# GpSimd makes all lower halves of the first 89 expert-up tiles, and VectorE passes each on behind its own step of expert choice

## The chip, the cores and the metric

The kernel runs on one core of a Trainium2 chip. The metric is the device time of one execution in microseconds (us). The kernel before took 4111.89 us (median of 3 runs, 4111.05 to 4112.73).

Five engines of the core work side by side: TensorE (PE; its weight loads are shown as PEld), VectorE (DVE), ScalarE (ACT), GpSimd (POOL), and SyncE (SP), which here only issues transfers. They meet at semaphores.

## The reference, cut to what matters

Four layers in a row, over 256 tokens of width 1024. Each is a mixer (RWKV-7 and pooling twice, a gated linear recurrence, latent attention) followed by a PEER feed-forward with 16384 experts. Only the feed-forward is touched by the change:

```
q = (h @ peer_q).reshape(B, S, 8, 2, 128)
scores = jnp.einsum('bshpd,hpkd->bshpk', q, peer_keys)
s, i = lax.top_k(scores, 16)                       # two lists of 16 for each head
cand_s = s[..., 0, :, None] + s[..., 1, None, :]   # 256 pair sums for each head
top_s, sel = lax.top_k(cand_s, 16)
gate = softmax(top_s)
act = gelu(einsum('td,ted->te', hx, u_sel))        # expert up
out = einsum('te,ted->td', gx * act, v_sel)        # expert down
```

The kernel does not gather the chosen experts. It multiplies the tokens by all 16384 rows of `peer_u`, in 128 tiles of 128 experts, and sets the unchosen ones to zero by a gate.

## The kernel before, in words

A weight tile of 128 x 1024 fp32 (512 KB) passes through four places. SP loads it into one of four `raw` buffers. ACT rounds it to `t_hi` (L707, the upper half). DVE or POOL makes the remainder `t_lo = raw - t_hi` (the lower half; L1195 on DVE, L617 on POOL). PE multiplies both. `t_hi` and `t_lo` have two buffers each, so the upper half of tile k starts once PE is through with tile k-2.

For the first 95 of the 128 expert-up tiles of a layer PE runs `merged`: 8 matmuls of 512 columns with `t_hi` (L2059), a wait for the lower half, then 8 matmuls of 256 columns with `t_lo` (L2067). Tile k needs a free PSUM bank too, that is, the sum of tile k-2 taken by DVE (L1780, semaphore `taken`).

Beside it, during the first 88 tiles, DVE chooses the experts: 44 steps for each of two halves of the tokens, one step to a tile. Steps 0 to 15 look for the largest 16 of 128 scores (instructions with one input); steps 16 and 17 form the pair sums (L1760, `tensor_tensor` over 1024 elements); steps 18 to 29 look for the largest 16 of 256 sums; step 30 prepares the softmax (L1831 to L1835, four short instructions); steps 31 to 42 are four look-ups, each of a comparison (L1768), a product (L1771) and a reduction (L1772); step 43 divides by the sum (L1843, short). In every step DVE first takes the sum of tile k-2 (`sum_of_tile`), then does the step (`choose`), then sees to a lower half (`lower_of_tile`).

Of the 88 tiles beside the choice, POOL makes the lower halves of the odd ones and DVE those of the even ones. PE waits on `lo_by_pool` for a tile of POOL's, and on `lo_done` for one of DVE's. `lo_done` counts all tiles in order, and SP waits on it before it loads the tile four further on. So DVE passes a tile of POOL's on: it waits for `lo_by_pool` and then raises `lo_done` by a tiny memset into `mark` (L1783). Behind the choice, POOL sets part of the arena to ones (L625) and makes gate columns (L631); DVE makes gate columns too (L1869).

Of the kernel before, what the change touches and what calls it, by code (L numbers as in the profile page):

```python
# [25 lines left out]
P = 128  # L26
# [3 lines left out]
TT = T // P  # L30
# [103 lines left out]
RANK_KEYS, PAIRS, RANK_PAIRS, SOFT, LOOK_UP, CHOSEN = 0, 16, 18, 30, 31, 43  # L134
STEPS = 44
LATE = TT * STEPS + 7
POOL_LOWERS = TT * STEPS // 2


def by_pool(k):  # L140

    return k % 2 == 1 and k < TT * STEPS
SMALL = {"mix0": 64, "mix1": 128, "mix2": 144, "mix3": 176}
NORMS_BEFORE = {"out0": 1, "out1": 3, "lout": 6, "wo": 8}
HSPLIT = {"ffn0": 3, "ffn1": 6, "ffn2": 9, "ffn3": 13, "wo": 11}
# [24 lines left out]
def in_loops(eng, name, a, b, body):  # L170

    tiles_in_loops(eng, SEGS[name][0] + a, b - a, lambda n, j, k, i: body(n, j, k + a, i))
# [63 lines left out]
def build(nc, x_in_dram, w_tiles, u_tiles, v_tiles, params, consts, lora, lru_w, mla_w, mla_uv, keys_t, pool_inv,  # L236
          positions, out):
    with ExitStack() as ctx:
        def sb(name, shape, dt=F32):
            return ctx.enter_context(nc.sbuf_tensor(name, shape, dt))  # L240

        def sem(name):
            return ctx.enter_context(nc.semaphore(name))
# [6 lines left out]
        x = sb("x", [P, DC, T])  # L250
        h_both = sb("h_both", [P, DC, 2, T], F32R)
        h_hi, h_lo = h_both[:, :, 0, :], h_both[:, :, 1, :]
        mark = sb("mark", [P, 1])
        par = sb("par", [P, NPAR])
        cst = sb("cst", [P, 4, P])
        mods = sb("mods", [P, 48])
# [35 lines left out]
        def act_slot(k, i):  # L292

            if i is None:
                return act_at[:, k // EB, :, k % EB, :]
            return act_at[:, bass.ds(i + k // EB, 1), :, k % EB, :].rearrange("p b q t -> p (b q) t")
# [6 lines left out]
        def by_quads(v):  # L303

            return v.rearrange("p (q t) -> p q t", t=4)
# [100 lines left out]
        lo_done = sem("lo_done")  # L406
        lo_by_pool = sem("lo_by_pool")
# [190 lines left out]
        def _(pool):  # L598
# [12 lines left out]
            def lower_halves(l):  # L611

                first = SEGS[f"u{l}"][0]
                for k in range(1, TT * STEPS, 2):
                    j = first + k
                    pool.wait_ge(hi_done, j + 1)
                    pool.tensor_tensor(t_lo[:, j % SPL, :], raw[:, j % RAW, :], t_hi[:, j % SPL, :].bitcast(F32),  # L617
                                       ALU.subtract).then_inc(lo_by_pool, 1)
# [42 lines left out]
            for l in range(4):  # L661
# [26 lines left out]
                pool.wait_ge(h_split, DC * HSPLIT[f"ffn{l}"])  # L688
                pool.dma_start(tk["keys"], keys_t[l]).then_inc(keys_in, 16)
                lower_halves(l)  # L690
                middle_hots(l)
                if l < 3:
# [494 lines left out]
        def _(dve):  # L1187
# [4 lines left out]
            def lower(n, j, name):  # L1192

                dve.wait_ge(hi_done, n + 1)
                tts(t_lo[:, j % SPL, :], raw[:, j % RAW, :], t_hi[:, j % SPL, :].bitcast(F32),  # L1195
                    ALU.subtract).then_inc(lo_done, 1)
# [577 lines left out]
            def sum_of_tile(l, k):  # L1774

                j = SEGS[f"u{l}"][0] + k
                if k >= 2:
                    dve.wait_ge(copied, LATE * l + k - 1)
                    slot = act_slot(k - 2, None)
                    tts(slot, by_quads(ps[:, j % 2, 0:T]), slot, ALU.add).then_inc(taken, 1)  # L1780
                if k and by_pool(k - 1):
                    dve.wait_ge(lo_by_pool, POOL_LOWERS * l + k // 2)
                    dve.memset(mark[:, :], 0.0).then_inc(lo_done, 1)  # L1783

            def lower_of_tile(l, k):

                if not by_pool(k):
                    lower(SEGS[f"u{l}"][0] + k, SEGS[f"u{l}"][0] + k, f"u{l}")

            def choose(l):  # L1790
# [11 lines left out]
                for tt in range(TT):  # L1802
                    for k in range(STEPS):
                        sum_of_tile(l, STEPS * tt + k)
                        if k < PAIRS:
                            if k % 4 == 0:
# [32 lines left out]
                        else:  # L1839
# [3 lines left out]
                            tts(e[:, 2], e[:, 2], tk["den"][:, 1, :].unsqueeze(2).broadcast_to([P, HEADS, TOPK]),  # L1843
                                ALU.mult).then_inc(chosen, 1)
                        lower_of_tile(l, STEPS * tt + k)
                a = TT * STEPS
                for k in range(a, a + 4):
                    sum_of_tile(l, k)
                    lower_of_tile(l, k)
                sel_out(1)  # L1850

            def gates(l):
# [34 lines left out]
                for k in range(TT * STEPS + 4, LATE + 2):  # L1887
                    sum_of_tile(l, k)
                    lower_of_tile(l, k)
                    if k == TT * STEPS + 4:  # L1890
                        dve.wait_ge(sel_ready, TT * (l + 1))
                        columns(0)
                    elif k == TT * STEPS + 5:
                        rows(0)
# [116 lines left out]
        def _(pe):  # L2011
# [37 lines left out]
            def merged(l, a, b):  # L2049

                name, first = f"u{l}", SEGS[f"u{l}"][0]

                def step(n, j, k, i):
                    pe.wait_ge(hi_done, n + 1)
                    pe.wait_ge(taken, k + (TAKEN[name] - 1))
                    hi = t_hi[:, j % SPL, :].rearrange("p (c m) -> p c m", c=DC)
                    lo = t_lo[:, j % SPL, :].rearrange("p (c m) -> p c m", c=DC)
                    for c in range(DC):
                        mm(ps[:, j % 2, :], hi[:, c, :], h_both[:, c, :, :].rearrange("p a t -> p (a t)"),  # L2059
                           start=(c == 0), stop=False)  # L2060
                    if by_pool(j - first):
                        at = POOL_LOWERS * l + (j - first) // 2 + 1
                        pe.wait_ge(lo_by_pool, at if i is None else i * 2 + at)
                    else:
                        pe.wait_ge(lo_done, n + 1)
                    for c in range(DC):
                        ins = mm(ps[:, j % 2, 0:T], lo[:, c, :], h_hi[:, c, :], start=False, stop=(c == DC - 1))  # L2067
                    ins.then_inc(tile_used, 1)
                in_loops(pe, name, a, b, step)
# [637 lines left out]
```

## Time and profile before

| | before |
|---|---|
| median of 3 runs | 4111.89 us |
| the profiled execution | 4110.32 us |
| its span | 4108.5 us |
| PE busy | 3973.6 us (97%) |
| DVE busy | 3062.8 us (75%) |
| ACT busy | 2336.6 us (57%) |
| POOL busy | 949.3 us (23%) |
| mean granted TensorE clock | 0.981 of full speed |

The 1.8 us between span and execution time lie outside the span. PE is the engine that sets the time; a share of busy time says nothing of a single stage, though, so the rows below are taken from the stage of the expert-up tiles. In layer 0 this lies between 294 and 575 us of the span; it comes four times.

### The profile page before, as it was taken

The page shows a single profiled execution, that of the slowest core. Times are in us where ns is not written, and L with a number is a line of the kernel's source. Part 1 is how long each engine was busy: PE and PEld are TensorE (multiplying, and loading weights), DVE is VectorE, ACT ScalarE, POOL GpSimd, SP SyncE. Part 2 cuts the span into 40 slices and gives each one's busy share as a digit, 9 for nine tenths or more (in the row PEclk, how much of TensorE's full clock was granted, in tenths as well). Part 3 has the DMA queues.
Part 4 walks back from the last instruction along what each step waited for, and adds up shares of the span by engine and source line. Part 5 has one row for each costly group of instructions (what it writes and reads, how often), then busy time and mean ns, then how long its engine had stood idle before and what let it go on. Part 6 is the DMA issues. An engine that isn't in the chain of part 4 may idle for free.

```text
span 4108.5 us, 76965 instructions
## 1 busy us (share of the span) xinstructions
PE 3973.6 (97%) x27046; PEld 3531.8 (86%) x27046; DVE 3062.8 (75%) x5383; ACT 2336.6 (57%) x4303; POOL 949.3 (23%) x646
## 2 busy tenths in 40 slices
PE   6999999999999999999998999999998999999999
PEld 6888889888889888988888988998887798898887
DVE  6758889767565888986766688987775578897555
ACT  4246578544534656854456566875454456686554
POOL 0104455000010444510000244531000034452000
PEclk9999999999999999999998999999998999999999
DMA  8345543878514554377853555358882255534664
GB/s 285 124 134 184 187 157 114 271 246 290 172 49 134 179 184 162 113 258 243 290 175 110 176 184 185 123 173 296 284 286 108 83 169 184 179 117 151 193 192 156
DMA packets 203683, 749.41 MB, mean 182 GB/s; under 512 B 22704, under 2 KB 23856, under 8 KB 202192
## 3 DMA queue, kind: packets, MB, share of 16 engines
q1 hardware_dynamic: 178416, 646.51, 47.1%
q0 software_dynamic: 25056, 100.15, 7.7%
q8 instruction: 125, 2.05, 0.2%
q14 instruction: 86, 0.70, 0.1%
HBM read 745.52 MB, written 1.05 MB: 182 GB/s over the span
## 4 chain that ended last, share of the span: by engine, by line
PE 88%; DVE 7%; ACT 3%; issue 1%; DMA 1%; POOL 1%; SPq 0%; DVEq 0%; ACTq 0%
PE ps L2059 15%; PE ps L2497 11%; PE ps L2504 11%; PE ps L2500 11%; PE ps L2067 8%; PE ps L2031 6%; PE ps L2032 6%; PE ps L2038 6%; PE ps L2480 6%; PE ps L2206 2%; DVE t_lo L1195 1%; ACT t_hi L707 1%; PE ps L2074 1%; DMA raw<-w_tiles 1%; PE ps L2455 1%
## 5 line engine op out<-in xcount | busy, mean ns | idle before, releaser
L707 ACT CAST t_hi<-raw 128x1024 fp32r<-128x1024 f32 x1180 | 1243.3, 1054 | 1004.6 <-PE ps L2504 694.4
L1195 DVE TENSOR_TENSOR t_lo<-raw,t_hi 128x1024 fp32r<-128x1024 f32 x1004 | 1229.3, 1225 | 686.2 <-ACT t_hi L707 667.8
L2059 PE MATMUL ps<-h_both,t_hi 128*128 128x512 f32 x3040 | 769.0, 395 | 10.9 <-DVE arena L1780 10.9
L2059 PEld LDWEIGHTS ps<-h_both,t_hi 128*128 128x128 f32 x3040 | 549.8, 190 | 111.2 <-issue 11.6
L2031 PE MATMUL ps<-h_both,t_hi 128*128 128x256 f32 x2304 | 603.7, 298 | 36.8 <-DVE h_both L1327 17.5
L617 POOL TENSOR_TENSOR t_lo<-raw,t_hi 128x1024 fp32r<-128x1024 f32 x176 | 453.6, 2577 | 744.0 <-ACT t_hi L707 744.0
L2032 PE MATMUL ps<-h_both,t_hi 128*128 128x256 f32 x2304 | 579.4, 287 | 0.0
L2497 PE MATMUL ps<-t_hi,h_both 128*128 128x512 f32 x2048 | 548.0, 389 | 5.4 <-DVE h_both L1919 5.4
L2504 PE MATMUL ps<-t_lo,h_both 128*128 128x512 f32 x2048 | 547.4, 389 | 0.0
L2500 PE MATMUL ps<-t_hi,h_both 128*128 128x512 f32 x2048 | 547.3, 389 | 0.0
L2031 PEld LDWEIGHTS ps<-h_both,t_hi 128*128 128x128 f32 x2304 | 451.2, 196 | 50.9 <-issue 34.6
L2497 PEld LDWEIGHTS ps<-t_hi,h_both 128*128 128x128 f32 x2048 | 383.9, 188 | 85.4 <-issue 6.1
L2067 PEld LDWEIGHTS ps<-h_both,t_lo 128*128 128x128 f32 x3040 | 412.2, 191 | 48.7 <-POOL t_lo L617 13.1
L2032 PEld LDWEIGHTS ps<-h_both,t_hi 128*128 128x128 f32 x2304 | 452.8, 197 | 1.2 <-issue 1.0
L2500 PEld LDWEIGHTS ps<-t_hi,h_both 128*128 128x128 f32 x2048 | 384.4, 188 | 79.9
L2504 PEld LDWEIGHTS ps<-t_lo,h_both 128*128 128x128 f32 x2048 | 384.4, 188 | 79.8
L2067 PE MATMUL ps<-h_both,t_lo 128*128 128x256 f32 x3040 | 428.4, 284 | 6.3 <-POOL t_lo L617 3.9
L631 POOL TENSOR_SCALAR oh<-cst,sel 128x128 f32<-128x128 f32 x256 | 340.1, 1335 | 261.5 <-PE ps L2480 261.5
L1130 ACT COPY arena<-ps 128x256 f32<-128x256 f32 x380 | 141.7, 373 | 438.2 <-PE ps L2067 438.1
L2038 PE MATMUL ps<-h_both,t_lo 128*128 128x256 f32 x2200 | 309.2, 283 | 0.0
L609 POOL DMA_DIRECT2D oh<-w_tiles x160 | 85.1, 532 | 867.9 <-DVE arena L1310 507.6
L2038 PEld LDWEIGHTS ps<-h_both,t_lo 128*128 128x128 f32 x2200 | 284.6, 192 | 0.0
(304 smaller groups left out, 4562.2 us busy)
## 6 DMA issues: line engine op xcount, KB each, us to landing
raw<-u_tiles SPq DMA_DIRECT2D x512, 512.0 KB, 3.3
raw<-v_tiles SPq DMA_DIRECT2D x512, 512.0 KB, 4.3
raw<-w_tiles SPq DMA_DIRECT2D x188, 512.0 KB, 3.6
oh<-w_tiles POOLq DMA_DIRECT2D x160, 512.0 KB, 4.8
arena<-w_tiles SPq DMA_DIRECT2D x16, 512.0 KB, 3.7
arena<-keys_t POOLq DMA_DIRECT2D x4, 1024.0 KB, 5.1
arena<-mla_w POOLq DMA_DIRECT2D x1, 4096.0 KB, 14.7
arena<-lora POOLq DMA_DIRECT2D x2, 1280.0 KB, 8.4
```

The source lines that it names most:

```text
L617: pool.tensor_tensor(t_lo[:, j % SPL, :], raw[:, j % RAW, :], t_hi[:, j % SPL, :].bitcast(F32), ALU.subtract).then_inc(lo_by_pool, 1)
L631: ins = pool.tensor_scalar(hot_cols[m % 2][:, q, :], iota, sel[:, 1, t:t + 1], sel[:, 2, t:t + 1], ALU.is_equal, ALU.mult)
L707: act.copy(t_hi[:, j % SPL, :], raw[:, j % RAW, :]).then_inc(hi_done, 1)
L1195: tts(t_lo[:, j % SPL, :], raw[:, j % RAW, :], t_hi[:, j % SPL, :].bitcast(F32), ALU.subtract).then_inc(lo_done, 1)
L2031: mm(o, hi[:, c, :], h_hi[:, c, :], start=(m == 0), stop=False)
L2032: mm(o, hi[:, c, :], h_lo[:, c, :], start=False, stop=False)
L2038: ins = mm(o, lo[:, c, :], h_hi[:, c, :], start=False, stop=(c == DC - 1))
L2059: mm(ps[:, j % 2, :], hi[:, c, :], h_both[:, c, :, :].rearrange("p a t -> p (a t)"), start=(c == 0), stop=False)
L2067: ins = mm(ps[:, j % 2, 0:T], lo[:, c, :], h_hi[:, c, :], start=False, stop=(c == DC - 1))
L2497: mm(ps[:, 2 + 2 * tt + half, :], wa_hi[:, b, tt * P:(tt + 1) * P], t_hi[:, j % SPL, cols], start=one, stop=False)
L2500: mm(ps[:, 2 + 2 * tt + half, :], wa_lo[:, b, tt * P:(tt + 1) * P], t_hi[:, j % SPL, cols], start=False, stop=False)
L2504: ins = mm(ps[:, 2 + 2 * tt + half, :], wa_hi[:, b, tt * P:(tt + 1) * P], t_lo[:, j % SPL, cols], start=False, stop=last)
```

## The change: who makes the lower halves, and where DVE passes them on

POOL makes the lower halves of tiles 0 to 88, and DVE none of them. The memset that raises `lo_done` for tile k-1 moves from the front of step k (behind the taken sum) to its end, at the place where the lower half was made. It rotates over four elements of `mark`, and each of the 89 tiles has one. PE waits on `lo_by_pool` for all of the first 89 tiles.

```
-POOL_LOWERS = TT * STEPS // 2
+POOL_LOWERS = TT * STEPS + 1
 def by_pool(k):
-    return k % 2 == 1 and k < TT * STEPS
+    return k < POOL_LOWERS
...
             def lower_halves(l):
                 first = SEGS[f"u{l}"][0]
-                for k in range(1, TT * STEPS, 2):
+                for k in range(POOL_LOWERS):
                     j = first + k
                     pool.wait_ge(hi_done, j + 1)
                     pool.tensor_tensor(t_lo[:, j % SPL, :], raw[:, j % RAW, :], t_hi[:, j % SPL, :].bitcast(F32),
...
                     tts(slot, by_quads(ps[:, j % 2, 0:T]), slot, ALU.add).then_inc(taken, 1)
+
+            def lower_of_tile(l, k):
+
                 if k and by_pool(k - 1):
-                    dve.wait_ge(lo_by_pool, POOL_LOWERS * l + k // 2)
-                    dve.memset(mark[:, :], 0.0).then_inc(lo_done, 1)
-
-            def lower_of_tile(l, k):
-
+                    dve.wait_ge(lo_by_pool, POOL_LOWERS * l + k)
+                    dve.memset(mark[:, k % 4:k % 4 + 1], 0.0).then_inc(lo_done, 1)
                 if not by_pool(k):
                     lower(SEGS[f"u{l}"][0] + k, SEGS[f"u{l}"][0] + k, f"u{l}")
...
                     if by_pool(j - first):
-                        at = POOL_LOWERS * l + (j - first) // 2 + 1
-                        pe.wait_ge(lo_by_pool, at if i is None else i * 2 + at)
+                        at = POOL_LOWERS * l + (j - first) + 1
+                        pe.wait_ge(lo_by_pool, at if i is None else i * 4 + at)
```

POOL's row of the program in layer 0, between the load of the keys (L689) and the memsets behind the choice:

```order
-L617 TENSOR_TENSOR t_lo<-raw,t_hi 128x1024 x44
+L617 TENSOR_TENSOR t_lo<-raw,t_hi 128x1024 x89
 L624 MEMSET arena 128x64x4
 L625 MEMSET arena 128x8192
```

44 lower halves have become 89 in each layer; what stands behind them is unchanged.

DVE's rows before in the look-ups of the first half of the tokens (L1768, L1771 and L1772 are the steps, L1780 the sums taken, L1195 the lower halves, L1783 the marks):

```order
608 L1768 TENSOR_TENSOR arena<-arena,cst 128x1024
609 L1780 TENSOR_TENSOR arena<-ps,arena 128x64x4
610 L1783 MEMSET mark 128x1
611 L1771 TENSOR_TENSOR arena<-arena 128x1024
612 L1195 TENSOR_TENSOR t_lo<-raw,t_hi 128x1024
613 L1780 TENSOR_TENSOR arena<-ps,arena 128x64x4
614 L1772 TENSOR_REDUCE arena<-arena 128x64
615 L1780 TENSOR_TENSOR arena<-ps,arena 128x64x4
616 L1783 MEMSET mark 128x1
617 L1768 TENSOR_TENSOR arena<-arena,cst 128x1024
```

And the same place with the change (the mark is now L1786):

```order
607 L1768 TENSOR_TENSOR arena<-arena,cst 128x1024
608 L1786 MEMSET mark 128x1
609 L1780 TENSOR_TENSOR arena<-ps,arena 128x64x4
610 L1771 TENSOR_TENSOR arena<-arena 128x1024
611 L1786 MEMSET mark 128x1
612 L1780 TENSOR_TENSOR arena<-ps,arena 128x64x4
613 L1772 TENSOR_REDUCE arena<-arena 128x64
614 L1786 MEMSET mark 128x1
615 L1780 TENSOR_TENSOR arena<-ps,arena 128x64x4
```

L1195 is gone from every second step, and each step ends with a mark behind its own work.

## Rows read from the trace of the kernel before

**Rows 1.** The page, busy time: engine, us, share of the span, instructions.
```profile
PE 3973.6 (97%) x27046; PEld 3531.8 (86%) x27046; DVE 3062.8 (75%) x5383; ACT 2336.6 (57%) x4303; POOL 949.3 (23%) x646
```

**Rows 2.** The waits of PE: who waited for whom, us in total, times, longest.
```profile
PE ps L2059 <- DVE arena L1780: 10.9, 4, 2.7
...
PE ps L2067 <- POOL t_lo L617: 3.9, 16, 0.3
```

**Rows 3.** Timeline of undisturbed tiles: start us, length us, instruction, [idle before <-releaser].
```profile
314.96 1.70 PEld L2059 LDWEIGHTS ps<-h_both,t_hi 128*128 128x128 f32 x8
...
316.70 1.13 PEld L2067 LDWEIGHTS ps<-h_both,t_lo 128*128 128x128 f32 x8
...
317.75 1.70 PEld L2059 LDWEIGHTS ps<-h_both,t_hi 128*128 128x128 f32 x8
...
318.05 1.23 DVE L1195 TENSOR_TENSOR t_lo<-raw,t_hi 128x1024 fp32r<-128x1024 f32 x1
...
318.34 1.05 ACT L707 CAST t_hi<-raw 128x1024 fp32r<-128x1024 f32 x1
...
319.48 2.41 POOL L617 TENSOR_TENSOR t_lo<-raw,t_hi 128x1024 fp32r<-128x1024 f32 x1 [3.17 <-ACT t_hi L707]
```

**Rows 4.** Timeline: POOL's lower halves of tiles 3, 15 and 87 of layer 0.
```profile
308.30 2.40 POOL L617 TENSOR_TENSOR t_lo<-raw,t_hi 128x1024 fp32r<-128x1024 f32 x1 [11.16 <-ACT t_hi L707]
...
341.82 2.41 POOL L617 TENSOR_TENSOR t_lo<-raw,t_hi 128x1024 fp32r<-128x1024 f32 x1 [3.17 <-ACT t_hi L707]
...
547.31 2.40 POOL L617 TENSOR_TENSOR t_lo<-raw,t_hi 128x1024 fp32r<-128x1024 f32 x1 [2.71 <-ACT t_hi L707]
```

**Rows 5.** Line L617 in layer 0: count, min/median/max ns, first and last start.
```profile
L617 POOL TENSOR_TENSOR t_lo<-raw,t_hi x44: 2360/2412/3400, 294.8 to 547.3; 128x1024 fp32r<-128x1024 f32 x44
```

**Rows 6.** Timeline of a look-up: a DVE product, then a lower half of POOL's.
```profile
398.09 1.22 DVE L1771 TENSOR_TENSOR arena<-arena 128x1024 f32<-128x1024 f32 x1
398.22 3.35 POOL L617 TENSOR_TENSOR t_lo<-raw,t_hi 128x1024 fp32r<-128x1024 f32 x1 [3.03 <-ACT t_hi L707]
...
401.62 1.01 PEld L2067 LDWEIGHTS ps<-h_both,t_lo 128*128 128x128 f32 x8 [0.63 <-POOL t_lo L617]
```

**Rows 7.** Timeline of the next look-up: POOL first, then a DVE comparison.
```profile
404.28 2.40 POOL L617 TENSOR_TENSOR t_lo<-raw,t_hi 128x1024 fp32r<-128x1024 f32 x1 [2.71 <-ACT t_hi L707]
...
404.34 3.42 DVE L1768 TENSOR_TENSOR arena<-arena,cst 128x1024 f32<-128x1024 f32 x1
```

**Rows 8.** Groups of DVE by shape, 294 to 574 us: count, busy us, mean ns, idle before.
```profile
L1768 DVE TENSOR_TENSOR arena<-arena,cst 128x1024 f32<-128x1024 f32 x8 | 14.1, 1768 | 0.2
...
L1760 DVE TENSOR_TENSOR arena<-arena 128x1024 f32<-128x1024 f32 x4 | 4.9, 1220 | 0.1
...
L1835 DVE CAST arena<-arena 128x256 f32<-128x256 uint32 x2 | 0.6, 294 | 0.1
...
L1833 DVE TENSOR_SCALAR arena<-arena 128x128 uint32<-128x128 uint32 x2 | 0.4, 220 | 0.0
```

**Rows 9.** Lines L1780 and L1772 in layer 0: count, min/median/max ns.
```profile
L1780 DVE TENSOR_TENSOR arena<-ps,arena x94: 405/420/426, 304.6 to 573.3; 128x256 f32<-128x256 f32 x94
...
L1772 DVE TENSOR_REDUCE arena<-arena x8: 1208/1213/1218, 392.6 to 544.6; 128x64 f32<-128x1024 f32 x8
```

**Rows 10.** Timeline: two waits of PE for DVE, and transposes between two tiles.
```profile
427.66 1.02 PEld L2067 LDWEIGHTS ps<-h_both,t_lo 128*128 128x128 f32 x8 [0.23 <-DVE t_lo L1195]
...
428.62 0.35 PEld L2466 LDWEIGHTS ps<-cst,arena 128*128 128x128 f32 x3
...
439.48 1.02 PEld L2067 LDWEIGHTS ps<-h_both,t_lo 128*128 128x128 f32 x8 [0.47 <-DVE t_lo L1195]
```

**Rows 11.** Timeline behind the choice: a memset of POOL's and two DVE instructions.
```profile
560.90 6.95 POOL L625 MEMSET arena<- 128x8192 f32 x1
...
562.71 5.29 DVE L1869 TENSOR_SCALAR oh<-cst,sel 128x128 f32<-128x128 f32 x2
```

**Rows 12.** DMA issues of the page: KB each, median us from issue to landing.
```profile
raw<-u_tiles SPq DMA_DIRECT2D x512, 512.0 KB, 3.3
```

More of the change, by code:

```diff
@@ L252, in build @@
         h_hi, h_lo = h_both[:, :, 0, :], h_both[:, :, 1, :]
-        mark = sb("mark", [P, 1])
+        mark = sb("mark", [P, 4])
         par = sb("par", [P, NPAR])
```

## The prediction, made before the changed kernel ran

> **What bounds the kernel now.** I read the busy times first: PE is busy for 97% of the span [rows 1], so a change away from PE counts only where PE waits, or where PE is made to wait. The list of PE's waits comes second. In the expert-up tiles it is short: 3.9 us in 16 waits for lower halves of POOL's, and one wait of at most 2.7 us in each layer for a sum taken by DVE [rows 2]. So DVE's 75% is no bound there, and freeing DVE is worth little by itself.
>
> The timeline gives the beat. An undisturbed tile takes PE 317.75 - 314.96 = 2.79 us, and it wants its lower half 316.70 - 314.96 = 1.74 us after its start [rows 3]. The tile behind those two starts at 317.75 + 2.79 = 320.54 and wants its lower half at 322.28. POOL delivers at 319.48 + 2.41 = 321.89, which is 0.39 us ahead. That slack is all there is: a lower half cannot start earlier, since the upper half waits for the buffer of the tile two before.
>
> What the stage loses already: POOL's lower halves of tiles 7 and 15, four pairs of tiles apart, start (341.82 - 319.48) / 4 = 5.585 us a pair apart, which is two beats [rows 3, 4]. From tile 3 to tile 87 there are 42 pairs, 42 x 5.585 = 234.6 us; the trace has 547.31 - 308.30 = 239.0 us [rows 4]. So 4.4 us a layer are lost, 0.3 of them to transposes that stay (L2466) [rows 10]. At most 4.1 us a layer, 16.4 us in all, can be won.
>
> Where they are lost is seen in the look-ups. L1771 on DVE starts at 398.09 and ends at 399.31. POOL's instruction starts at 398.22 and takes 3.35 us instead of 2.40: it ends at 401.57, 2.26 us behind the end of DVE's, and PE's weight loads wait 0.63 us for it [rows 6]. The other way round, L1768 starts at 404.34 while POOL works until 406.68; it takes 3.42 us instead of 1.22 and ends at 407.76, 1.08 us behind POOL [rows 7]. So a DVE `tensor_tensor` with both inputs in SBUF and POOL's lower half exclude each other for their whole length. L1780, whose one input lies in PSUM, and the reduction L1772 never stretch (at most 426 and 1218 ns) [rows 9].
>
> **The change part by part.** Removed from DVE: 45 lower halves of 1.23 us a layer, 55 us [rows 3]. Nothing waits for this time except at two places: PE waits 0.23 and 0.47 us for DVE's lower halves where DVE is behind [rows 10]. These 0.7 us a layer should go.
>
> Added to POOL: 45 lower halves of 2.41 us. POOL then works 2.41 us of each 2.79. In the steps with one-input instructions (0 to 15, 18 to 29) this costs nothing: ACT delivers an upper half each beat, POOL's start and end stay in the places they now have for odd tiles [rows 3], and 0.39 us is left. The cover is thin: anything over 0.39 us on POOL's instruction reaches PE.
>
> The price is paid where DVE needs what POOL now holds nearly always. I count exclusive time against PE's beat.
> - A look-up (three steps): three lower halves and two `tensor_tensor`s. With handovers 2 x 2.26 + 2 x 1.08 + 2.40, and 0.07 from semaphore to start: 9.15 us. PE needs 3 x 2.79 = 8.38. Excess 0.77; four look-ups 3.1 us.
> - The two pair-sum steps (L1760): 2 x (2.26 + 1.08) = 6.7, with a short cast of 0.29 (as L1835) ahead 7.0, against 5.6 [rows 8]. Excess 1.3, less the 0.4 of slack: 0.9.
> - Step 30: four short instructions, two of 0.22 and two of about 0.29 us (L1833 and L1835 are two of them) [rows 8], 1.0 us beside a lower half of 2.26: 3.3 against 2.8, less the slack: 0.1. They count only if short `tensor_scalar`s and casts are held too. The row nearest says so: two L1869 of 128 elements take 5.29 us and end at 568.00, just behind POOL's memset at 567.85 [rows 11]. That is a memset and not a lower half; I take it.
>
> Sum for one half of the tokens 4.1, for a layer 8.2, less the 4.1 lost now: +4.1 us. Four layers: **+16.4 us**. Lower bound for the price: DVE slips into POOL's pauses and PE never waits, -16.4 us. Upper bound: each of the 20 long `tensor_tensor`s a layer (8 L1768, as many L1771, 4 L1760 [rows 8]) delays PE by 2.41 + 1.22 - 2.79 = 0.84 us with no slack used, 16.8 a layer, less 4.1: +51 us. I take the middle one since it is counted with handovers that rows 6 and 7 show.
>
> The Trainium skill (SBUF — State Buffer, "Who interferes with whom") names the instructions that take the port pair shared with GpSimd: `tensor_tensor` with two SBUF inputs against a GpSimd instruction that reads SBUF, and copy, cast and `tensor_scalar` in their two-port modes, but not `tensor_reduce`. Rows 6, 7 and 9 agree for the first and the last; on casts no run here shows it yet. If it were wrong on the short instructions, the pair sums would cost 0.7, step 30 nothing and the look-ups 2.7 for each half of the tokens, and the sum would be 2 x 3.4 - 4.1 = 2.7 us a layer, +11 us.
>
> Moved: the mark. Before, DVE passed a tile of POOL's on behind the sum of the next step; now behind the step itself, where L1195 stood. In the undisturbed step that is at 318.05, 3.09 us behind PE's start of the tile at 314.96 [rows 3]. What hangs on it is SP's load of the tile four further on. ACT wants that tile behind PE's start of the tile three further on, 3 x 2.79 + (318.34 - 317.75) = 8.96 us behind the same start [rows 3]. Landing takes 3.3 us [rows 12], so about 2.6 us are left; without this cover each tile would be late by what is missing. The mark's wait is for the tile before the step's own, whose lower half ends early in the step; behind it on DVE queues the next sum, which PE wants a beat later. The memsets go into DVE's freed time. On PE, a register operation more stands ahead of the lower matmuls of even tiles; odd tiles have it now and keep the same beat.
>
> Unmoved: behind the choice POOL's memsets start on DVE's signal, so the wait of 2.7 us on L1780 [rows 2] stays; tile 88 changes hands with nothing beside it.
>
> The sum stands on the profiled execution, 4110.32 us, span 4108.5. It is 1.6 us under the median, so I add the difference to the median: 4111.9 + 16.4 = 4128.3.
>
> **The rivals.**
> 1. Exchange: the collisions cost as much as before, since L1195 no longer collides and DVE can catch up. For it: part of the present losses is L1195 against POOL or DVE behind [rows 10]. Against it: the exclusive time of two look-up steps is now 2.40 + 1.23 + 4/3 x 1.22 = 5.3 us, under the 5.6 of two beats; with the change it is 2/3 x 9.15 = 6.1. Time: 4112, within 8 us.
> 2. Faster: DVE, rid of 55 us a layer, is never behind and takes each `tensor_tensor` in POOL's pause of 2.79 - 2.41 = 0.38 us; POOL starts later by the rest, and slack and reduction steps catch it. PE then loses only the transposes. It decides if the exclusion costs POOL under 0.4 us a `tensor_tensor`. Against it: it cost 0.95 us in one pass (3.35 against 2.40) [rows 6]. Time: 4111.9 - 16.4 = 4095.5 at best, with half of it 4104.
> 3. Much slower: one-input searches are held too once POOL never rests, or DVE asks late each time and waits a full lower half, so that PE waits for the sum queued behind it (a step of 2.40 + 1.08 + 0.42 = 3.9 us). For it: one L1768 waited 2.2 us [rows 7]. If 16 look-up steps a layer last 3.9 - 2.79 = 1.1 us too long, and the pair sums as computed, it is 17.6 + 1.8 - 4.1 = 15.3 us a layer, 4173; half of them give 4138. Against it: POOL's median is 2412 ns with searches beside it [rows 5].
>
> **How the numbers follow.** Under 0.2% (8 us) this kernel's change can hardly be told from none. Forecast (+9 to +28 us) 0.66; rival 1 0.14; rival 2 0.10; rival 3 0.10. The predicted time is the forecast's, 4128. The range leaves out a tenth at either end: 4106 to 4143; the forecast's own range is 4121 to 4140. Faster 0.09, same 0.16, slower 0.75, with the small overlaps of the cases at 8 us.
>
> **What would show it.** Right: L617 x356 with a median still near 2.41 us and a mean of some 2.6; L1768 and L1771 with means of 1.8 us or more, L1195 down by 180; in the search steps beats of 2.79 us; PE's waits for POOL's lower halves in the look-ups and pair sums only, several times the 3.9 us of now; waits for L1195 nearly gone. Wrong: beats above 2.79 us in steps 0 to 15 (POOL too slow or a held search), waits of ACT for loads (the late mark), or a POOL median over 2.8 us.

## The result, and the profile after

The changed kernel takes 4127.44 us (median of 6 runs, 4124.77 to 4129.9), the kernel before 4110.66 (median of 6 runs, the three of above among them). The ratio is 1.0042, with a 95% interval from 1.0029 to 1.0055: slower. The profiled execution has a span of 4125.5 us, 17.0 more than before.

The page of the changed kernel, for comparison with [rows 1]:

```profile
PE 3982.2 (97%) x27046; PEld 3530.9 (86%) x27046; DVE 2916.2 (71%) x5383; ACT 2333.6 (57%) x4303; POOL 1416.7 (34%) x826
```

DVE works 147 us less and POOL 467 us more; PE runs the same 27046 matmuls. The list of PE's waits, for [rows 2]:

```profile
PE ps L2059 <- DVE arena L1780: 13.0, 12, 2.7
PE ps L2067 <- POOL t_lo L617: 12.6, 48, 0.3
```

48 waits for POOL's lower halves instead of 16, 12 in each layer; the waits for DVE's are gone; and eight short waits for a sum have joined the four of 2.7 us. These figures are PE's own idle time. The weight loads, which run ahead, wait longer (0.3 and 0.7 us in the look-up shown below).

Starts of POOL's lower halves of tiles 3, 30 and 87 in the timeline of layer 0, and line L617 there, for [rows 4, 5]:

```profile
310.52 2.41 POOL L617 TENSOR_TENSOR t_lo<-raw,t_hi 128x1024 fp32r<-128x1024 f32 x1 [0.38 <-ACT t_hi L707]
...
386.92 2.40 POOL L617 TENSOR_TENSOR t_lo<-raw,t_hi 128x1024 fp32r<-128x1024 f32 x1 [0.39 <-ACT t_hi L707]
...
553.65 2.45 POOL L617 TENSOR_TENSOR t_lo<-raw,t_hi 128x1024 fp32r<-128x1024 f32 x1 [0.33 <-ACT t_hi L707]
```
```profile
L617 POOL TENSOR_TENSOR t_lo<-raw,t_hi x89: 2360/2406/3397, 294.1 to 556.4; 128x1024 fp32r<-128x1024 f32 x89
```

From tile 3 to tile 87: 243.13 us, where 84 beats of 2.793 (half of the pair's 5.585) are 234.6. So 8.5 us are lost, against 4.4 before. That is +4.1 us a layer. The median of POOL's instruction has not moved: POOL is not slow, it is sometimes held. In the search steps it rests 0.38 or 0.39 us between two passes and PE loses nothing there.

The same can be measured with one ruler in every kernel: ACT's copies out of PSUM (L1130) start at a fixed distance behind the end of each tile. The time between the copies of two tiles, less 2.793 us for each tile, is what PE lost. In layer 1, in us:

```
                                tiles 2-87   pair sums   step 30 and   tiles    behind
                                in all       (16-17)     look-ups      43-50    tile 87
before                            4.25       0.53 0.52    1.33 1.31     0.71     5.1
after                             8.34       0.98 0.97    3.11 3.11     0.33     5.0
```

(Two numbers: the two halves of the tokens. The other search steps count 0.00 or 0.01 everywhere.) ACT's copy of tile 2 comes 0.17 us late behind other work of ACT's, in every kernel, and that is no loss of PE's: every loss "in all" is therefore 0.17 too low, and their differences are right. In these two kernels layers 0, 2 and 3 agree with layer 1 within 0.1 up to tile 87.

A look-up in the changed kernel, tiles 37 to 39 of layer 0 (DVE's L1768, L1771 and L1772; weight loads of PE show when the lower half was wanted), for [rows 6, 7]:

```profile
407.56 1.38 DVE L1768 TENSOR_TENSOR arena<-arena,cst 128x1024 f32<-128x1024 f32 x1
408.21 3.00 POOL L617 TENSOR_TENSOR t_lo<-raw,t_hi 128x1024 fp32r<-128x1024 f32 x1 [0.35 <-ACT t_hi L707]
...
410.35 1.94 DVE L1771 TENSOR_TENSOR arena<-arena 128x1024 f32<-128x1024 f32 x1
411.26 1.01 PEld L2067 LDWEIGHTS ps<-h_both,t_lo 128*128 128x128 f32 x8 [0.28 <-POOL t_lo L617]
...
413.26 1.21 DVE L1772 TENSOR_REDUCE arena<-arena 128x64 f32<-128x1024 f32 x1
414.61 1.00 PEld L2067 LDWEIGHTS ps<-h_both,t_lo 128*128 128x128 f32 x8 [0.72 <-POOL t_lo L617]
...
417.26 3.02 POOL L617 TENSOR_TENSOR t_lo<-raw,t_hi 128x1024 fp32r<-128x1024 f32 x1 [0.33 <-ACT t_hi L707]
```

I call what DVE and POOL take turns at the port. The comparison ends at 408.94 and POOL's pass, due at 408.21, ends only at 411.21. The product asks at 410.35, gets the port at 411.21 and holds POOL's next pass. By the reduction, POOL's pass is 0.72 us late for PE's loads. The look-up takes 417.26 - 408.21 = 9.05 us of port time; it was computed as 9.15, and PE needs 8.38, so it loses 0.67.

Where the look-ups begin, a short cast is held for a whole pass of POOL's:

```profile
386.92 2.40 POOL L617 TENSOR_TENSOR t_lo<-raw,t_hi 128x1024 fp32r<-128x1024 f32 x1 [0.39 <-ACT t_hi L707]
...
386.99 2.48 DVE L1835 CAST arena<-arena 128x256 f32<-128x256 uint32 x1
...
389.85 3.35 DVE L1768 TENSOR_TENSOR arena<-arena,cst 128x1024 f32<-128x1024 f32 x1
```
```profile
397.06 1.68 PEld L2059 LDWEIGHTS ps<-h_both,t_hi 128*128 128x128 f32 x8 [0.48 <-DVE arena L1780]
```

It took 0.29 us before [rows 8]. It asks 0.07 us behind POOL's start, and through the two instructions behind it PE waits for a sum.

### The profile page after: what moved, and what is told of

It reads as the page before. It is cut to its first block, busy times and chain, and to the rows that moved or that the text cites. A ratio compares the mean times of both kernels' runs of the same rounds, so it can differ in the third digit from the quotient of the medians.

```text
span 4125.5 us, 77317 instructions
## 1 busy us (share of the span) xinstructions
PE 3982.2 (97%) x27046; PEld 3530.9 (86%) x27046; DVE 2916.2 (71%) x5383; ACT 2333.6 (57%) x4303; POOL 1416.7 (34%) x826
## 4 chain that ended last, share of the span: by engine, by line
PE 84%; POOL 6%; DVE 4%; ACT 3%; issue 1%; DMA 1%; SPq 0%; DVEq 0%; ACTq 0%
PE ps L2059 12%; PE ps L2497 11%; PE ps L2504 11%; PE ps L2500 11%; PE ps L2067 7%; PE ps L2031 6%; POOL t_lo L617 6%; PE ps L2032 6%; PE ps L2038 6%; PE ps L2480 6%; PE ps L2206 2%; ACT t_hi L707 2%; DMA raw<-w_tiles 1%; PE ps L2074 1%; PE ps L2455 1%
## 5 line engine op out<-in xcount | busy, mean ns | idle before, releaser
L1195 DVE TENSOR_TENSOR t_lo<-raw,t_hi 128x1024 fp32r<-128x1024 f32 x824 | 1008.9, 1225 | 679.5 <-ACT t_hi L707 665.4
L617 POOL TENSOR_TENSOR t_lo<-raw,t_hi 128x1024 fp32r<-128x1024 f32 x356 | 921.5, 2596 | 303.8 <-ACT t_hi L707 303.8
L2067 PEld LDWEIGHTS ps<-h_both,t_lo 128*128 128x128 f32 x3040 | 409.0, 190 | 62.9 <-POOL t_lo L617 37.5
L1130 ACT COPY arena<-ps 128x256 f32<-128x256 f32 x380 | 141.4, 372 | 453.5 <-PE ps L2067 453.4
L1780 DVE TENSOR_TENSOR arena<-ps,arena 128x256 f32<-128x256 f32 x380 | 161.1, 424 | 297.0 <-ACT arena L1130 295.3
```

## The experiments

All times are medians beside runs of the kernel before on the same chip; ratios are to that, with their 95% interval. Loss is the ruler above, tiles 2 to 87 of layer 1.

**The two-input instructions taken away, from the changed kernel.** The pair sums and the first two instructions of each look-up become reductions over as many elements. Their buffers are set to zero first, in the idle time in front of the choice.

```
-                return tts(tk["cand"][:, h].rearrange(...), two(val, 0, h)..., two(val, 1, h)..., ALU.add)
+                return dve.tensor_reduce(e[:, 0, h], c, AX.X, ALU.add)
...
-                if step == 0:
-                    return tts(eq, hat[:, w, h]..., iota..., ALU.is_equal)
-                if step == 1:
-                    return tts(eq, eq, two(idf, w, h)..., ALU.mult)
                 return dve.tensor_reduce(e[:, w, h], eq, AX.X, ALU.add)
```

> The changed kernel, but the 20 long tensor_tensors of the choice in each layer (pair sums, comparisons and products of the look-ups) are replaced by reductions over as many elements, which have one input; the chosen experts are therefore not the right ones. Theory (DVE's two-input instructions and POOL's lower halves exclude each other): POOL still makes all 89 lower halves, but nothing holds it; PE keeps the beat of 2.79 us in the pair sums and look-ups, and of the 8.5 us lost in a layer some 8 go: 4127.4 - 32 = 4095 us. POOL's lower halves keep a maximum near 2.5 us. Rival (POOL or the late mark is too slow by itself, or PE's waits on the other semaphore cost): the time stays above 4120.

Measured: 4095.7 us, ratio 0.9960 (0.9947 to 0.9974). Loss 0.28. POOL makes all its 356 lower halves and is never held:

```profile
L617 POOL TENSOR_TENSOR t_lo<-raw,t_hi 128x1024 fp32r<-128x1024 f32 x356 | 856.0, 2406 | 336.8 <-ACT t_hi L707 336.8
```

So without them neither POOL's rate, nor the late mark, nor PE's waits on the other semaphore cost anything. The whole loss hangs on which instructions DVE runs beside POOL.

**The same, from the kernel before.**

> The kernel before with the same replacement of the 20 long tensor_tensors by reductions of one input (the chosen experts are not the right ones). Theory: the 3.6 us a layer that the look-ups and pair sums lose to the exclusion go, the 0.7 us where DVE is behind stay: 4110.7 - 13 to 14 = 4097 us, so that the two divisions of the lower halves end within 5 us of each other. Rival (the changed kernel is slower by its greater use of POOL alone): it stays 16 us ahead of the changed kernel with the same replacement.

Measured: 4096.89 us, ratio 0.9966 (0.9954 to 0.9978), loss 0.58, with 0.71 at tiles 43 to 50. Without the two-input instructions both divisions of the work end together, with the changed one ahead by the 0.4 us a layer that DVE's lateness cost.

**POOL alone in the searches, every other tile elsewhere.** Two semaphores by the tile's parity take the place of `lo_by_pool`, so that any tile can be given to either engine; DVE raises one of them for its own lower halves too, and passes every tile on by the mark.

```
-    return k < POOL_LOWERS
+    kk = k % STEPS
+    return k < POOL_LOWERS and (kk < 16 or 18 <= kk < 30 or k % 2 == 1)
...
-        lo_by_pool = sem("lo_by_pool")
+        lo_made = [sem(f"lo_made{k}") for k in range(2)]
```

> The changed kernel, but in the steps with two-input instructions (16, 17, 30 to 43 of each half of the tokens) DVE makes the lower halves of the even tiles again; POOL makes all in the search steps. PE waits on one of two semaphores by the tile's parity. Theory: all of the loss lies in those steps, so the time is that of the kernel before, less the 0.7 us a layer where DVE was behind: 4110.7 - 3 = 4108 us. Rival (the loss lies in POOL's use over all steps): about 63% of the tiles keep it, and the time is 4120 or more.

Measured: 4103.07 us, ratio 0.9980 (0.9971 to 0.9989), loss 1.79. The searches cost nothing, as expected; but it is 5 us faster than I expected. The look-ups lose 0.44 instead of 1.33 with the same division as before, so something else in them was better. Two differences are left there: the place of the mark, and the two semaphores. The next run has the first alone.

**The mark alone: the kernel before with the mark behind the step.** This came last, to settle that.

```
-                if k and by_pool(k - 1):
-                    dve.wait_ge(lo_by_pool, POOL_LOWERS * l + k // 2)
-                    dve.memset(mark[:, :], 0.0).then_inc(lo_done, 1)
-
             def lower_of_tile(l, k):
 
+                if k and by_pool(k - 1):
+                    dve.wait_ge(lo_by_pool, POOL_LOWERS * l + k // 2)
+                    dve.memset(mark[:, :], 0.0).then_inc(lo_done, 1)
                 if not by_pool(k):
```

> The kernel before with only the mark moved behind the step; POOL still makes the odd tiles and DVE the even ones. It does one part of the change alone. Theory (in front of a look-up step the mark's wait for POOL's lower half keeps DVE idle for up to a microsecond; behind the step it has passed): the look-ups lose 0.4 to 0.5 us in place of 1.3 for each half of the tokens and the pair sums 0.4 in place of 0.5, as where POOL made all tiles of the searches alone; 8 us in all, 4103 to 4105 us. Rival (the mark's place costs nothing or the loads come late): 4110 or more.

Measured: 4102.13 us, ratio 0.9977 (0.9968 to 0.9986), loss 1.94: pair sums 0.35, look-ups 0.51 and 0.50, tiles 43 to 50 0.40. One half of the change was a gain of 2.3 us a layer. In the kernel before DVE stood at the mark until POOL was through and only then did its step, so the step ran into DVE's own next lower half. In [rows 6], POOL ends at 401.57. The next step of the kernel before, in the same timeline:

```profile
401.61 1.22 DVE L1772 TENSOR_REDUCE arena<-arena 128x64 f32<-128x1024 f32 x1 [1.09 <-issue]
401.63 0.06 DVE L1783 MEMSET mark<- 128x1 f32 x1
402.86 1.23 DVE L1195 TENSOR_TENSOR t_lo<-raw,t_hi 128x1024 fp32r<-128x1024 f32 x1
```

The reduction starts only when POOL is through, though it needs nothing of it. DVE's lower half follows late, and the next comparison asks 0.06 us behind POOL's start and is held for the whole pass [rows 7]. In this run the reduction starts 1.2 us before POOL's end, and the comparison comes ahead of POOL:

```profile
398.89 3.34 POOL L617 TENSOR_TENSOR t_lo<-raw,t_hi 128x1024 fp32r<-128x1024 f32 x1 [3.03 <-ACT t_hi L707]
...
401.09 1.21 DVE L1772 TENSOR_REDUCE arena<-arena 128x64 f32<-128x1024 f32 x1
...
404.29 1.22 DVE L1768 TENSOR_TENSOR arena<-arena,cst 128x1024 f32<-128x1024 f32 x1
404.94 2.83 POOL L617 TENSOR_TENSOR t_lo<-raw,t_hi 128x1024 fp32r<-128x1024 f32 x1 [2.72 <-ACT t_hi L707]
```

**The mark back in front, in the changed kernel.** Its two lines move from the end of the step back behind the sum; nothing else changes.

> The changed kernel with the mark back in front of each step, behind the sum taken. Theory (the loss is the exclusion alone): the mark's place costs nothing, 4127 us within 4. Rival (the late mark delays loads or sums): towards 4111. A third way: DVE now waits at the mark for POOL's lower half in the saturated look-ups and then asks for the port, which is the moment it is free; the same sum, so again 4127.

Measured: 4121.9 us, ratio 1.0016 (1.0007 to 1.0026), loss 7.10: pair sums 0.76 and 0.77, look-ups 2.71 and 2.70. The expectation of "the same" fails by 1.2 us a layer, in the direction opposite to the run above. The groups of DVE by shape show what differs, first in the changed kernel, then here:

```profile
L1771 DVE TENSOR_TENSOR arena<-arena 128x1024 f32<-128x1024 f32 x8 | 18.4, 2302 | 0.0
L1768 DVE TENSOR_TENSOR arena<-arena,cst 128x1024 f32<-128x1024 f32 x8 | 15.0, 1880 | 0.0
```
```profile
L1768 DVE TENSOR_TENSOR arena<-arena,cst 128x1024 f32<-128x1024 f32 x8 | 26.9, 3366 | 1.5 <-issue 1.5
L1771 DVE TENSOR_TENSOR arena<-arena 128x1024 f32<-128x1024 f32 x8 | 23.7, 2962 | 0.0
```

With the mark in front, DVE's comparison asks for the port when POOL's pass has already begun, in every look-up, and the waits are 1.5 and 0.7 us longer on average. Yet a look-up costs the same. POOL's passes of layer 0 in this run:

```profile
392.61 8.65 POOL L617 TENSOR_TENSOR t_lo<-raw,t_hi 128x1024 fp32r<-128x1024 f32 x3 [0.39 <-ACT t_hi L707]
...
401.67 8.65 POOL L617 TENSOR_TENSOR t_lo<-raw,t_hi 128x1024 fp32r<-128x1024 f32 x3 [0.40 <-ACT t_hi L707]
...
410.73 8.65 POOL L617 TENSOR_TENSOR t_lo<-raw,t_hi 128x1024 fp32r<-128x1024 f32 x3 [0.41 <-ACT t_hi L707]
```

They are 9.06 us apart, and 9.05 in the changed kernel. So the port time of a look-up does not depend on which of the two comes late, and there the third way of the expectation held. What differs is one event in each half of the tokens. In the changed kernel DVE comes late into the first look-up (its comparison takes 3.35 us) and early into the others (1.38), and between the two a pass of POOL's more is held. From POOL's pass of tile 31 to that of tile 43 of layer 1 it is 36.62 us there and 36.21 here: 0.4 us a half. The pair sums lose 0.2 us less, and together that is the 1.2 us a layer.

**POOL's lower half in two instructions.**

```
-                    pool.tensor_tensor(t_lo[:, j % SPL, :], raw[:, j % RAW, :], ...).then_inc(lo_by_pool, 1)
+                    for half in (slice(0, D // 2), slice(D // 2, D)):
+                        ins = pool.tensor_tensor(t_lo[:, j % SPL, half], raw[:, j % RAW, half], ...)
+                    ins.then_inc(lo_by_pool, 1)
```

> The changed kernel, but each of POOL's lower halves is made by two instructions of 512 columns. A DVE instruction can then go between them. Theory (what counts is the sum of exclusive time against the beat, not how long one wait lasts): no gain in the look-ups; what the second start costs POOL comes on top wherever POOL is full, and if two halves take over 2.79 us together, all steps are late: 4127 to 4140. Rival (the loss comes from waits for whole passes, which shorter ones would cut): below 4122.

Measured: 4147.12 us, ratio 1.0084 (1.0067 to 1.0101), 7 us past the expectation's upper end. Loss 12.41: pair sums 1.64 and 1.66, look-ups 4.46 and 4.48, searches 0.01.

```profile
L618 POOL TENSOR_TENSOR t_lo<-raw,t_hi 128x512 fp32r<-128x512 f32 x712 | 977.0, 1397 | 264.6 <-ACT t_hi L709 264.2
```
```profile
L618 POOL TENSOR_TENSOR t_lo<-raw,t_hi x712: 1260/1297/2329, 294.6 to 3604.8; 128x512 fp32r<-128x512 f32 x178
```
```profile
PE ps L2069 <- POOL t_lo L618: 29.2, 71, 1.4
```

Shorter passes do not help. By the medians two of them take 2 x 1.297 = 2.59 us, 0.19 more than one of 2.41, which is 0.56 for the three passes of a look-up; a look-up loses 1.11 us, 0.44 more than the 0.67 of the changed kernel. POOL's own longer time is enough to account for that. Whether more handovers cost something of themselves is not shown.

**The casts as reductions over one element each,** in the changed kernel.

```
-                            link(cp(hat, hatu))
+                            link(dve.tensor_reduce(hat.rearrange("p w h k -> p (w h k)"),
+                                                   hatu.rearrange("p w h k -> p (w h k)").unsqueeze(2), AX.X, ALU.max))
```

> The changed kernel with the two casts (ahead of the pair sums and in step 30) made by reductions over one element each, which give the same values. In the trace of the changed kernel the cast of step 30 took 2.48 us, held by POOL, DVE came late into the look-ups and PE waited 0.4 to 0.5 us for a sum. Theory: this goes, 0.5 us in each half of the tokens, and up to 0.3 in the pair sums: 4127.4 - 4 to 6 = 4122 us, and the loss from tile 3 to 87 in a layer falls from 8.5 to about 7.3 us. Rival (the casts' wait is covered by DVE's idle time): no change.

Measured: 4126.18 us, ratio 1.0031 (1.0019 to 1.0042); loss 7.45: look-ups 2.69 and 2.68, pair sums 0.96 and 0.95. The reduction over the same 256 elements is no longer held for a pass:

```profile
L1836 DVE TENSOR_REDUCE arena<-arena 128x256 f32<-128x256 uint32 x2 | 0.8, 420 | 0.1
```

So the held cast of step 30 costs 0.42 us a time, 3.4 us in all; the cast in front of the pair sums costs 0.02. The 0.42 is not the cast's own wait but the change from late to early behind it: from the pass of tile 31 to that of tile 43 of layer 1 it is 36.20 us here, as with the mark in front, where the cast was held just as long (2.38 us). The sum of the two is less than the 4 to 6 us I expected, and the medians alone (1.3 us apart) would not have shown it.

**Only the pair sums taken away,** as in the first experiment.

> The changed kernel with only the pair sums replaced by reductions of one input (the chosen experts are not the right ones). It sizes one term of the sum: 0.9 us for each half of the tokens, so 4127.4 - 7 = 4120 us and 1.8 us a layer less; the loss of the look-ups stays. Rival (both losses share one slack, so that one grows when the other goes): less than half of that.

Measured: 4117.59 us, ratio 1.0016 (1.0007 to 1.0026); loss 6.38: pair sums 0.00, look-ups 3.09 and 3.11 as in the changed kernel. The term is 0.98 for each half of the tokens, and the two losses do not share a slack.

**POOL beside the reductions.** This is the version that the accounting points to.

```
-    return k < POOL_LOWERS
+    kk = k % STEPS
+    return k < POOL_LOWERS and (kk < 16 or 18 <= kk < 30 or kk in (33, 36, 39, 42))
```

> As the run before, but in the look-ups POOL makes only the lower half of the tile of each reduction step (33, 36, 39, 42), and DVE the others; in steps 16, 17, 30 and 43 DVE makes them. Theory: POOL's pass then lies beside the reduction and is over when the next comparison asks; exclusive time in three steps 2 x 1.22 + 2 x 1.23 + 2.4 = 7.3 of 8.4 us, DVE's own 3 x 1.7 + 2 x 1.23 = 7.6. Nearly all of the 4.1 us a layer go: 4110.7 - 13 to 16 = 4096 us, faster than both kernels. Rival (DVE is then the engine that is late, in steps 16, 17 and 43): 4105 to 4112.

Measured: 4097.37 us, ratio 0.9965 (0.9951 to 0.9978); run again, 4094.92 us, 0.9954 (0.9941 to 0.9968). Loss 0.19 and 0.18: nothing in pair sums and look-ups, 0.33 for the transposes. Beside the kernel before it is faster by 0.35 and 0.46%, and the changed kernel is slower than that one by 0.42%. POOL makes 65 lower halves a layer:

```profile
L625 POOL TENSOR_TENSOR t_lo<-raw,t_hi 128x1024 fp32r<-128x1024 f32 x260 | 625.1, 2404 | 567.5 <-ACT t_hi L715 567.5
```

What was expected of the rerun, beside the next experiment:

> The version with POOL beside the reductions once more, on the same chip as the run before: 4097 us. All theories expect the same.

**The gate columns ahead of POOL's memset,** on top of it. What is left in the stage is the 5 us behind tile 87. In the version with POOL beside the reductions DVE's two gate columns are held by POOL's memset, as in [rows 11].

```
                     lower_of_tile(l, k)
+                    if k == a + 1:
+                        dve.wait_ge(sel_ready, TT * l + 1)
+                        for t in range(POOL_FROM):
+                            ts(hot_cols[0][:, t, :], iota, sel[:, 1, t:t + 1], sel[:, 2, t:t + 1], ALU.is_equal, ALU.mult)
                 sel_out(1)
...
                         dve.wait_ge(sel_ready, TT * (l + 1))
-                        columns(0)
```

> The version with POOL beside the reductions, and DVE's first two gate columns moved from the step behind the choice, where POOL's memset of 6.95 us holds them for 5.3 us and PE waits 2.7 us for the sum queued behind, to the tile before the memset starts (tile 89; nothing of POOL's runs there). Theory (a memset of POOL's excludes a tensor_scalar of DVE's, and the wait for the sum is on PE's path): the four waits of 2.7 us go, 4097.4 - 11 = 4087 us. Rival (PE then waits for something else behind the memset, such as DVE's rows or POOL's columns): 4092 to 4097.

Measured: 4079.26 us, ratio 0.9919 (0.9905 to 0.9932). The gain over the version beside it is 15.7 us, where 11 were expected. The loss behind tile 87 falls from 4.9 to 0.6 us. Windows of the stretch behind the choice (busy time of PE, PEld, DVE, ACT and POOL, then granted clock, DMA share, GB/s), without and with:

```profile
552.00:580.00 28.00, 25.29 (x155) 22.61 (x154) 20.69 (x24) 16.88 (x37) 12.95 (x7) 0.94 0.50 160
567.70:570.90 3.20, 3.05 (x7) 2.48 (x8) 3.20 (x5) 1.59 (x5) 3.20 (x3) 0.50 0.27 68
```
```profile
552.00:580.00 28.00, 28.00 (x192) 25.92 (x191) 20.62 (x29) 20.68 (x46) 13.99 (x8) 1.00 0.59 188
```

The wait of 2.7 us was followed by 3.4 us at half of the clock (0.50 is 1.2 of 2.4 GHz), which makes 0.94 over the 28 us; without the wait the clock stays at 1.00. That is 0.06 x 28 = 1.7 us more, together 4.4 us a layer and 17.6 in four; the ruler has 17.7. The medians gained 15.7, the spans of the two profiled executions 18.3 (4097.3 and 4079.0). And within the memset, DVE's `tensor_scalar`s were held while its `tensor_tensor`s with two SBUF inputs were not:

```profile
560.29 6.94 POOL L633 MEMSET arena<- 128x8192 f32 x1
560.95 1.23 DVE L1203 TENSOR_TENSOR t_lo<-raw,t_hi 128x1024 fp32r<-128x1024 f32 x1 [0.53 <-ACT t_hi L715]
562.09 5.29 DVE L1882 TENSOR_SCALAR oh<-cst,sel 128x128 f32<-128x128 f32 x2
```

## Why the prediction was right

The forecast was 4128 us and the measured median 4127.4. The forecast was +16.4; the medians are 16.8 apart and the spans 17.0. Up to tile 87, where the mechanism works, the ruler has 4 x (8.34 - 4.25) = 16.4. The place, the mechanism and the size of a look-up were right; that the sum fits to a tenth is in part luck, as the terms show.

- **The beat and the slack.** Right. In the searches POOL rests 0.38 to 0.39 us between passes and PE loses nothing.
- **The most that could be won,** 4.1 us a layer. Right: the version with POOL beside the reductions gets 4.1 (loss 0.19 for 4.25).
- **Exclusion as the mechanism.** Right: with the two-input instructions gone, a loss of 8.34 becomes 0.28, from the changed kernel, and 4.25 becomes 0.58, from the one before.
- **The terms.** For each half of the tokens: pair sums 0.9 computed, 0.98 measured; look-ups with step 30 3.2 computed (3.1 and 0.1), 3.11 measured. A look-up's port time 9.15 computed, 9.05 measured. Within the second term two errors cancel: step 30 costs 0.42 and not 0.1, since the held cast sends DVE late into the first look-up, and the four look-ups alone cost 2.69 and not 3.1. In the first term two cancel as well: the cast that was counted costs 0.02, and without it 0.7 was computed where 0.96 is lost; and 7.0 less 5.6 is 1.4 and not 1.3.
- **Short instructions.** I counted them because of [rows 11] and weighed a rule of the Trainium skill with it, that casts and `tensor_scalar`s can take the port pair shared with GpSimd (SBUF — State Buffer, "Who interferes with whom"). The trace agrees on casts: 2.48 us for 0.29. On `tensor_scalar`s beside a lower half it decides nothing: the two of step 30 took 0.22 us each every time, and in layer 0 they start at 386.60 and 386.74, in POOL's pause before 386.92. What I had as the sum without them, +11, is not what it would have been: without the casts' hold the loss is 7.45 a layer, which is 4 x (7.45 - 4.25) = +12.8.
- **The mark.** This step was wrong. I cost it at nothing because loads have 2.6 us left, and no run showed an expert-up load late. But I looked only at what hangs behind the mark and not at what it did in its old place, a wait in front of the step. By itself the move gains 2.3 us a layer with alternating tiles and costs 1.2 us a layer with POOL on all. The gain is already in the sum, since the trace that I corrected had the loss of the old place in it and the new sum was made afresh from port time; as a separate term it was missing. The cost is in it only by the step-30 term that turned out larger: a look-up's port time is the same at both places.
- **The rest of the span.** In the stage of layers 1 to 3 the first to the last tile take 4.0 us more each, in layer 0 2.8: there the 2.7 us wait was not followed by the dip of the clock in the changed kernel's execution. The remaining 2.2 us lie ahead of the first changed instruction. I take them for the scatter between two executions (the kernel before alone spans 4107.17 to 4112.73); that is not shown. So the 17.0 of the span is 16.4 up to tile 87, 1.8 less behind it and 2.2 more ahead of it.

**The rivals.** Exchange (4112) fell: collisions rose from 4 to 8 us a layer. Faster (4095.5 at best) fell with its condition: a held pass of POOL's took 2.96 to 3.39 us for 2.40, not under 0.4 more. Its 4.1 us a layer are there to be won, but by keeping the two apart, as in the version with POOL beside the reductions. Much slower (4138 and up) did not come, and its price was wrong, not only its condition: with the mark in front DVE asks late in every look-up and PE does wait for the sum behind it, and still a look-up takes 9.06 us, not the 8.38 + 2 x 1.1 = 10.6 of that rival.

## What to carry to other kernels

GpSimd's pass and VectorE's two-input instruction take turns, so add up their times against the beat of the engine that bounds, step by step, before moving work from one to the other. An average says nothing here: the searches had room for all of it and the look-ups for a third. A better division gives GpSimd the steps in which VectorE runs instructions with one input, and that version took 0.35 to 0.46% less time than the kernel before.

A wait that costs nothing where it ends can cost where it stands: look at what the engine would have done meanwhile.

## What the runs showed of the hardware that was not expected

- A look-up cost 9.05 us of port time whether VectorE's comparison came ahead of GpSimd's pass or behind its start (9.06 with the mark in front). A change from one order to the other cost 0.4 us once.
- A pass of POOL's in two instructions of half the length took 2 x 1.397 = 2.79 us on average beside DVE, against 2.60 for one (by the medians 2.59 against 2.41), and PE lost 12.4 us a layer against 8.3.
- A wait of PE of 2.7 us cost 4.4 us where the granted clock fell to half behind it (0.94 over 28 us, 1.00 without the wait). The dip does not follow every such wait: behind tile 87 the loss is 5.0 us in layers 1 to 3 of the changed kernel and 3.57 in layer 0.
- A memset of POOL's held a `tensor_scalar` of DVE's over 128 elements (5.29 us for two; 0.34 us each on average over the 248 of the run with the early columns) and did not hold a `tensor_tensor` with two SBUF inputs (1.23 us). The Trainium skill (SBUF — State Buffer, "Who interferes with whom") says that a two-input DVE instruction contends only with a GpSimd instruction that reads SBUF. The trace agrees.
